# Gathered expert blocks of 64 tokens with two slots each, summed on TensorE as two 64-column tiles

## What is computed

```python
eidx = jnp.take_along_axis(cidx, fi, axis=-1)              # (token, head, 16): rows in u and v
g = jax.nn.softmax(fv, axis=-1)
act = jax.nn.gelu(jnp.einsum('thkd,td->thk', u[eidx], xb).astype(jnp.float32), approximate=False)
return jnp.einsum('thk,thkd->td', (g * act).astype(xb.dtype), v[eidx])
```

## Time and profile before

| | us |
|---|---|
| median of 3 runs | 5584.86 (5583.2 to 5591.33) |
| span of the profiled execution | 5599.6 |
| TensorE, VectorE, GpSimd, ScalarE busy | 4306.3, 3537.3, 2480.1, 1216.0 |
| last stage | 4931 to 5593 |

### The profile page before, as it was taken

One profiled execution on the slowest core, in us unless ns is written; L12 is line 12 of the kernel. 1 busy time (PEld: TensorE's weight loads), 2 busy tenths in 40 slices (PEclk: granted clock), 3 DMA queues, 4 the chain that ended last, 5 costly groups with the idle time before them and its releaser, 6 DMA issues. The chain is left out here.

```text
span 5599.6 us, 50197 instructions
## 1 busy us (share of the span) xinstructions
PE 4306.3 (77%) x15868; PEld 2641.6 (47%) x15868; DVE 3537.3 (63%) x7830; ACT 1216.0 (22%) x3039; POOL 2480.1 (44%) x2215
## 2 busy tenths in 40 slices
PE   7956886578577988689677676968678798767777
PEld 6334775543333765263334565554344476223333
DVE  4055638866677546686666848966667754854544
ACT  2042311121332112120422311121242211111111
POOL 0000010166555544546565332456555554477776
PEclk9975997689789999799898888988889899888888
DMA  4311631389787987889889966688888798799999
GB/s 141 118 60 41 229 124 61 118 294 349 269 272 267 334 284 272 278 308 371 290 292 323 339 203 199 203 286 323 306 274 274 264 359 281 249 361 409 409 409 361
DMA packets 579390, 1484.67 MB, mean 265 GB/s; under 512 B 60104, under 2 KB 251176, under 8 KB 572616
## 3 DMA queue, kind: packets, MB, share of 16 engines
q0 software_dynamic: 307200, 1115.82, 55.2%
q1 hardware_dynamic: 258968, 331.39, 17.8%
q10 hardware_dynamic: 12960, 34.26, 1.6%
HBM read 1435.37 MB, written 45.93 MB: 265 GB/s over the span
## 5 line engine op out<-in xcount | busy, mean ns | idle before, releaser
L2721 PE MATMUL duo<-vring,diag 128*128 128x512 f32 (+1 forms) x2976 | 1509.2, 657 | 401.1 <-DMA vring<-in_peer_v,eidx 173.2
L2593 POOL DMA_INDIRECT uring<-in_peer_u,eidx x981 | 1140.5, 1163 | 1112.3 <-DVE uring L2629 658.0
L2674 POOL DMA_INDIRECT vring<-in_peer_v,eidx x1024 | 1134.0, 1107 | 1067.0 <-PE duo L2721 472.7
L2721 PEld LDWEIGHTS duo<-vring,diag 128*128 128x128 f32 (+1 forms) x2976 | 589.6, 208 | 1197.3 <-issue 944.6
L2629 DVE SCALAR_TENSOR_TENSOR uring<-uring,xr 128x1024 f32<-128x1024 f32 x795 | 958.9, 1221 | 204.6 <-DMA uring<-in_peer_u,eidx 178.8
L689 PE MATMUL duo<-wx,xT 128*128 128x512 f32 (+3 forms) x1440 | 605.1, 578 | 32.9 <-PEq L133 32.1
L2754 DVE SCALAR_TENSOR_TENSOR x_tok<-vring,wt,x_tok 128x1024 f32<-128x1024 f32 x296 | 385.0, 1301 | 97.0 <-DMA vring<-in_peer_v,eidx 70.4
L2702 ACT ACTIVATE diag<-ident,wt 128x128 f32<-128x128 f32 x728 | 269.8, 395 | 748.4 <-PE duo L2721 678.8
L689 PEld LDWEIGHTS duo<-wx,xT 128*128 128x128 f32 (+1 forms) x1440 | 238.9, 176 | 385.8 <-issue 383.1
L2629 DVE SCALAR_TENSOR_TENSOR uring<-uring,duo 128x1024 f32<-128x1024 f32 x201 | 245.4, 1221 | 264.4 <-DMA uring<-in_peer_u,eidx 263.9
L533 PE MATMUL duo<-xT,wx 128*128 128x264 f32 (+1 forms) x1536 | 357.6, 397 | 36.5 <-ACT newcols L556 30.6
(11 more groups left out here) (472 smaller groups left out, 5283.8 us busy)
## 6 DMA issues: line engine op xcount, KB each, us to landing
wx<-in_w_in SPq DMA_DIRECT2D x32, 2048.0 KB
wx<-in_w_in SPq DMA_DIRECT2D x48, 1024.0 KB, 8.3
wm<-in_w_in SPq DMA_DIRECT2D x32, 1024.0 KB, 10.4
wm<-in_w_branch_a SPq DMA_DIRECT2D x32, 1024.0 KB, 11.6
wq<-in_peer_wq SPq DMA_DIRECT2D x32, 1024.0 KB, 8.7
tokm<-tout ACTq DMA_DIRECT2D x64, 256.0 KB
eb<-decays SPq DMA_DIRECT2D x32, 512.0 KB, 4.5
s_h<-in_state_ssm SPq DMA_DIRECT2D x16, 1024.0 KB, 8.3
```

The costliest lines, as they stand in the source:

```text
L2593: pool.indirect_dma_start(out=E.rings.urows[K % E.ur], out_offset=None, in_=table, in_offset=bass.IndirectOffsetOnAxis(ap=E.tiles[q][3][:, ...
L2674: pool.indirect_dma_start(out=E.rings.vrows[K % E.vr], out_offset=None, in_=table, in_offset=bass.IndirectOffsetOnAxis(ap=E.tiles[q][3][:, ...
L2721: mm = pe.matmul(G.bank[6 + c][0:m, :], G.diag[:, R % DR, 0:m], E.rings.vrows[K % E.vr][:, c * BANK:(c + 1) * BANK], start=first, stop=las ...
```

## The change

A gathered block now holds 64 tokens and two of their slots: partition 64k + t has token t of the half tile and its slot number k of the pair. The two blocks that follow each other serve tokens 0 to 63 and 64 to 127 of the tile, so there are as many gathers of the same size as before. The matrix that TensorE multiplies with has 64 columns (`subsel`, two identities one above the other, scaled by the weights), which adds the two slots; the first block of a pair writes PSUM partitions 0 to 63, the second 64 to 127. A pair is issued at once, waits for both of its blocks, and frees them together. All sums are made so; `SHARES`, L2754 and the copies of the token rows into PSUM are gone. The indices and gates are dealt to this layout by four DMAs per tile behind each route (`routed`), and the token rows are loaded as two buffers of 64 tokens each held twice, both used by every tile. The samples' 8 slots keep their layout.

```diff
-UR, VR, DR = 5, 4, 4
+UR, VR = 5, 4
+PACK = 2
+SUB = P // PACK
+DEAL = SLOTS // PACK
+DR = 2 * PACK
...
+        @block.sync
+        def _(sp):
+            go = G.beside.by(sp, "SP")
+            G.ahead.fetch(sp, 0, *vectors)
+            for i, (t, n, heads, sc) in enumerate(units):
+                go(ends[i])
+                sp.wait_ge(sem("routed"), i + 1)
+                if t < NT:
+                    for j in range(PACK):
+                        for k in range(PACK):
+                            sp.dma_start(G.routed[k * SUB:(k + 1) * SUB, t, :, j * DEAL:(j + 1) * DEAL],
+                                         B.dealing[j * SUB:(j + 1) * SUB, :, k * DEAL:(k + 1) * DEAL]).then_inc(sem("dealt"), 16)
+                else:
+                    for a in range(PK // deals):
+                        sp.dma_start(G.eidx_s[a:P:PK // deals, :], S.es[:, 0, a * deals:(a + 1) * deals]).then_inc(sem("dealt"), 16)
+                        sp.dma_start(G.gate_s[a:P:PK // deals, :], S.gs[:, 0, a * deals:(a + 1) * deals]).then_inc(sem("dealt"), 16)
+            sp.wait_ge(sem("dealt"), dealt[-1])
...
+    def column(self, j):
+        return j % PACK * DEAL + j // PACK if self.dealt else j
+
+    def out(self, j):
+        return slice(j % PACK * SUB, (j % PACK + 1) * SUB) if self.dealt else slice(0, self.n)
...
@@ -2603,11 +2641,13 @@
 
     G = E.G
     for q, tile in enumerate(E.tiles):
-        if q >= 2:
-            yield E.first[q - 1] + 0.5
-        if E.k0 or q >= 2:
-            sp.wait_ge(G.dotted, E.k0 + (E.first[q - 1] if q >= 2 else 0))
-        sp.dma_start(G.xr[:, q % 2, :], tile[6]).then_inc(G.xrow[q % 2], 16)
+        for b, rows in zip(tile.buffers, tile.subs):
+            at = E.before(q, b)
+            if at is not None:
+                yield at + 1.5
+            if E.k0 or at is not None:
+                sp.wait_ge(G.dotted, E.k0 + (0 if at is None else at + 1))
+            sp.dma_start(G.xr[:, b, :], rows).then_inc(G.xrow[b], 16)
 
 
...
-            K = E.r0 + i
-            if j == 0:
-                dve.wait_ge(G.xrow[q % 2], 16 * (E.xr0[q % 2] + q // 2 + 1))
-            xr = G.xr[:, q % 2, :]
-            if q in E.copies and i >= E.copied:
-                xr = G.duo[q % 2][:].rearrange("p c n -> p (c n)")
-                dve.wait_ge(E.row_copied, E.copies.index(q) + 1)
+            tile = E.tiles[q]
+            K, b = E.r0 + i, tile.buffer(j)
+            if j < len(tile.buffers):
+                dve.wait_ge(G.xrow[b], 16 * E.loads(q, b))
             dve.wait_ge(E.rings.usems[K % E.ur], 16 * (K // E.ur + 1))
             row = E.rings.urows[K % E.ur]
-            dve.scalar_tensor_tensor(row, row, 1.0, xr, ALU.mult, ALU.mult,
+            dve.scalar_tensor_tensor(row, row, 1.0, G.xr[:, b, :], ALU.mult, ALU.mult,
                                      accum_out=G.pre[:, q % 2, j:j + 1]).then_inc(G.dotted, 1)
         if i - WEIGH_AFTER in E.ends:
             q, lo, hi = E.ends[i - WEIGH_AFTER]
+            tile = E.tiles[q]
             g = E.g0 + E.rank[(q, lo, hi)]
             dve.wait_ge(G.gelu, g + 1)
-            dve.tensor_tensor(G.wt[:, q % 2, lo:hi], G.pre[:, q % 2, lo:hi], E.tiles[q][4][:, lo:hi], ALU.mult).then_inc(G.weighed, 1)
+            dve.tensor_tensor(tile.slots_of(G.wt[:, q % 2], lo, hi), tile.slots_of(G.pre[:, q % 2], lo, hi), tile.gates_of(lo, hi),
+                              ALU.mult).then_inc(G.weighed, 1)
 
 
...
 
     G = E.G
-    copies = {max(E.first[q] - 3.7, E.copied + 0.3): q for q in E.copies}
-    for at in sorted([i + 1.0 for i in E.ends] + list(copies)):
-        yield at
-        if at in copies:
-            q = copies[at]
-            act.wait_ge(G.xrow[q % 2], 16 * (E.xr0[q % 2] + q // 2 + 1))
-            if q >= 2:
-                act.wait_ge(G.dotted, E.k0 + E.first[q - 1])
-            act.activation(G.duo[q % 2][:, 0, :], G.xr[:, q % 2, 0:BANK], ACT.Copy)
-            act.activation(G.duo[q % 2][:, 1, :], G.xr[:, q % 2, BANK:], ACT.Copy).then_inc(E.row_copied, 1)
-            continue
-        i = int(at) - 1
+    for i in sorted(E.ends):
+        yield i + 1.0
         q, lo, hi = E.ends[i]
         act.wait_ge(G.dotted, E.k0 + i)
         act.activation(G.pre[:, q % 2, lo:hi], G.pre[:, q % 2, lo:hi], ACT.Gelu).then_inc(G.gelu, 1)
...
 def sums_scalar(act, E):
 
     G = E.G
-    for v in range(E.n):
-        if not E.on_pe[v]:
-            continue
-        yield max(v + 1.0 - LEAD, E.ready(v))
-        q, j = E.slots[v]
-        K = E.p0 + E.rank_pe[v]
-        act.wait_ge(G.weighed, E.g0 + E.group(q, j) + 1)
-        if K >= DR:
-            act.wait_ge(G.summed, K - DR + 1)
-        sel = E.tiles[q][5]
-        m = sel.shape[1]
-        act.activation(G.diag[:, K % DR, 0:m], sel, ACT.Copy, scale=G.wt[:, q % 2, j:j + 1]).then_inc(G.diagged, 1)
+    for v in range(0, E.n, PACK):
+        yield max(v + PACK - LEAD, E.ready(v))
+        for i in range(v, v + PACK):
+            q, j = E.slots[i]
+            K = E.k0 + i
+            act.wait_ge(G.weighed, E.g0 + E.group(q, j) + 1)
+            if K >= DR:
+                act.wait_ge(G.summed, (K - DR) // PACK + 1)
+            sel = E.tiles[q].sel
+            act.activation(G.diag[:, K % DR, 0:sel.shape[1]], sel, ACT.Copy, scale=G.wt[:, q % 2, j:j + 1]).then_inc(G.diagged, 1)
 
 
 def sums_tensor(pe, E):
 
     G = E.G
-    for v in range(E.n):
-        if not E.on_pe[v]:
-            continue
-        yield v + 1.0
-        q, j = E.slots[v]
-        m = E.tiles[q][5].shape[1]
-        R, K = E.p0 + E.rank_pe[v], E.r0 + v
-        first, last = v == E.pe_first[q], v == E.pe_last[q]
-        if first and E.q0 + E.pe_tiles.index(q) > 0:
-            pe.wait_ge(G.xadd, E.q0 + E.pe_tiles.index(q))
-        pe.wait_ge(G.diagged, R + 1)
-        pe.wait_ge(E.rings.vsems[K % E.vr], 16 * (K // E.vr + 1))
+    for v in range(0, E.n, PACK):
+        yield float(v + PACK)
+        q, j0 = E.slots[v]
+        tile = E.tiles[q]
+        m = tile.sel.shape[1]
+        if j0 == 0 and E.q0 + q > 0:
+            pe.wait_ge(G.xadd, E.q0 + q)
+        pe.wait_ge(G.diagged, E.k0 + v + PACK)
+        for i in range(v, v + PACK):
+            K = E.r0 + i
+            pe.wait_ge(E.rings.vsems[K % E.vr], 16 * (K // E.vr + 1))
         for c in range(2):
-            mm = pe.matmul(G.bank[6 + c][0:m, :], G.diag[:, R % DR, 0:m], E.rings.vrows[K % E.vr][:, c * BANK:(c + 1) * BANK],
-                           start=first, stop=last, skip_group_check=True)
+            for i in range(v, v + PACK):
+                j = E.slots[i][1]
+                mm = pe.matmul(G.bank[6 + c][tile.out(j), :], G.diag[:, (E.k0 + i) % DR, 0:m],
+                               E.rings.vrows[(E.r0 + i) % E.vr][:, c * BANK:(c + 1) * BANK],
+                               start=j < (PACK if tile.dealt else 1), stop=j >= tile.slots - (PACK if tile.dealt else 1), skip_group_check=True)
         mm.then_inc(G.summed, 1)
 
 
 def sums_vector(dve, E):
 
     G = E.G
-    for v in range(E.n):
-        q, j = E.slots[v]
-        t, n = E.tiles[q][0:2]
-        K = E.r0 + v
-        last = v == E.pe_last.get(q)
-        if E.on_pe[v] and not last:
-            continue
-        yield v + 1.0
-        done = E.d0 + E.rank_dve[v]
-        if done:
-            dve.wait_ge(G.folded, done)
-        if last:
-            dve.wait_ge(G.summed, E.p0 + E.rank_pe[v] + 1)
-            if E.q0 + E.pe_tiles.index(q):
-                dve.wait_ge(G.xadd, E.q0 + E.pe_tiles.index(q))
-            for c in range(2):
-                xs = G.x[0:n, t, c * BANK:(c + 1) * BANK]
-                add = dve.tensor_tensor(xs, xs, G.bank[6 + c][0:n, :], ALU.add)
-            add.then_inc(G.xadd, 1)
-        else:
-            added = E.q0 + sum(E.pe_last[p] < v for p in E.pe_tiles)
-            if added and E.pe_last.get(q, v) < v:
-                dve.wait_ge(G.xadd, added)
-            dve.wait_ge(E.rings.vsems[K % E.vr], 16 * (K // E.vr + 1))
-            x = G.x[0:n, t, :]
-            dve.scalar_tensor_tensor(x, E.rings.vrows[K % E.vr], G.wt[:, q % 2, j:j + 1], x, ALU.mult, ALU.add).then_inc(G.folded, 1)
+    for q, tile in enumerate(E.tiles):
+        v = E.first[q] + tile.slots
+        yield float(v)
+        dve.wait_ge(G.summed, E.p0 + v // PACK)
+        if E.q0 + q:
+            dve.wait_ge(G.xadd, E.q0 + q)
+        for c in range(2):
+            xs = G.x[0:tile.n, tile.t, c * BANK:(c + 1) * BANK]
+            add = dve.tensor_tensor(xs, xs, G.bank[6 + c][0:tile.n, :], ALU.add)
+        add.then_inc(G.xadd, 1)
 
 
 DOTS = {"POOL": dots_pool, "SP": dots_sync, "DVE": dots_vector, "ACT": dots_scalar}
```

More of the change, by code:

```diff
@@ L2565, in later, with before, loads @@
     def later(self):
-        n = sum(self.on_pe)
-        return (self.k0 + self.n, self.g0 + len(self.ends), self.q0 + len(self.pe_tiles), self.p0 + n, self.d0 + self.n - n)
+        return self.k0 + self.n, self.g0 + len(self.ends), self.q0 + len(self.tiles), self.p0 + self.n // PACK
+    def before(self, q, b):
```

(19 more changed lines are left out.)

128 lines of the change are left out of this document (58 added, 70 removed).

## The result

The changed kernel takes 5920.16 us (5903.87 to 5930.16) against 5588.09 us of the kernel before on the same chip: ratio 1.0588, 95% interval 1.0565 to 1.0610, slower by 332 us. The forecast was 128 us and its range ended at 5810. The sign held; the size and the range didn't.

What follows compares the result with a forecast made beforehand. The prediction took no one engine as the bound throughout: TensorE, VectorE, alternating engines or DMA, by stage. Terms 99 - 72 + 16 + 18 + 72 - 5 = +128 us on 5585 gave 5713 us, range 5610 to 5810.

Steps and rivals of the forecast that it cites:

- What bounds each kind of stage: TensorE bounds late scores and mix; SSD and attention alternate engines on one tile; DMA bounds the last stage.
- the pair at 1.91 us: On TensorE, two 64-column tiles run side by side, so the sums of two slots take 1.91 us.
- TensorE stages, +99: Late scores, layer 2's early scores and late mix: all sums on TensorE cost +50, +5 and +44 us.
- Alternating stages, -72: SSD, attention and early mix: less sum work gives -20, -39 and -13, together -72 us, between -45 and -110.
- The sentence on the ring: SSD and attention: a block of four frees only with its pair, so the second gather has one slot less lead.
- Dealing, +16: After routes, SyncE's four small index DMAs hold up the end of four stages by about 4 us each, +16 us.
- Token rows, +18 (0 to 36): Six places where the second token-row load waits for the tile before, 3 us each, +18 us (0 to 36).
- Last stage, +72 for the port: Last stage: dots with both operands in SBUF lengthen GpSimd's gathers, a slot 2.88 us for 2.56, +72 us.
- Rival 1: Last stage: the shared read port costs nothing, as gathers waiting in the DMA engines absorb it; 5641 us, chance 0.12.
- rival 2: Last stage: dots lock into a bad phase with gathers, a slot up to 3.57 us; 5868 us, chance 0.12.
- The tail's -5: End of the last stage: 16 pairs take 28 us on TensorE alone, for 35 us side by side, -5 us.
- Rival 4: Sums on TensorE: the two column tiles run one after the other, 3.62 us a pair; 5916 us, chance 0.06.

Runs made afterwards that it cites:

- x1: The changed kernel with each token-row load written as two plain transfers of 64 rows instead of one [2, 64, 1024] transfer; ratio 1.0307 to the kernel before.
- x4: The kernel before without ScalarE's copies of the token rows to PSUM, so last-stage dots read both operands from SBUF; ratio 1.0009 to the kernel before.
- x5: The changed kernel with plain token-row loads and one row buffer moved from the dot products' ring to the sums' ring (4 to 5); ratio 1.0264.
- x3: The kernel before with all sums on TensorE, each a 128-column sum of its own, none on VectorE; ratio 1.0442 to the kernel before.
- the same-columns run: The changed kernel with plain token-row loads, both slots of a pair writing the same 64 output columns; ratio 1.0905 to the kernel before.

## Why the prediction was right or wrong

- **What bounds each kind of stage** and **the pair at 1.91 us**: right. (One reading was off, without effect: a DMA share of 1.03 isn't the most of that trace, weights reach 1.09 from 1086 to 1090.) In the late scores stage TensorE is busy 96.69 of 97.00 us, 25.2 more than in the earlier trace rows, 1.94 us for each of 13 pairs.

```profile
2148.30:2245.30 97.00, 96.69 (x474) 69.25 (x474) 0.00 (x0) 23.41 (x90) 22.96 (x26) 0.98 0.64 205
```

- **TensorE stages, +99**: +94.6 (late scores 48.6, the early one 4.4, late mix 41.6).
- **Alternating stages, -72**: -40.6, outside the bound of -45 (SSD -12.6 for -20, attention -36.7 for -39, early mix +8.7 for -13). For SSD and attention the mechanism was right and partly taken back by the ring: plain loads with four buffers (`x1`) give -49 in these stages against the kernel without PSUM copies (`x4`, same chip), and with five (`x5`, another chip, one buffer fewer for the dots) -86. In the early mix the sum itself has a gap: it takes 18 sums, 23 us, off VectorE and puts nothing on TensorE for the nine pairs that replace them, 17 us at 1.91. With the same sums on TensorE one by one (`x3`) these stages take 385.9 us for the 381.7 of `x4`.
- **Attention inputs and route stages**, whose sums were costed at 0: wrong. First route +31.6, attention inputs +13.0, the early route +6.9. The sentence on the ring ("gathers start two at a time and the second has one slot less of lead") named the cause, and I weighed it only where foreground work could cover it. It costs most in the first route stages, where TensorE has none. Of their +34.6 us with plain loads the fifth buffer takes 31 away; for the attention inputs and the early route no run separates the ring from the rest.
- **Dealing, +16**: the stage with layer 1's early route, whose sums and dots haven't begun, is 4.1 us longer (156.8 for 152.7 us), the 4 us forecast. In layer 2's, SyncE leaves the stage only 1.7 us behind the other engines, and in the other two it can't be told from the reload. The size fits where it can be read.
- **Token rows, +18 (0 to 36)**: the step that failed. "A load takes 4.6 to 9.8, median 7.1 us" was taken from transfers of 128 rows and applied to one of [2, 64, 1024]. It took 17 to 41 us until the dot that needed it, and it also held up the weights issued behind it ("so no weights wait" was wrong in the late halves' first stages, where the loads stand ahead of them). The term of 18 us cost 168 by its shape alone. With loads as I had costed them the waits are 38.8 us, at the upper end of 0 to 36 even so, and in four places and not six.
- **Last stage, +72 for the port**: wrong, zero. "If dots fall at random" failed ("landings jitter"): they lock to the gathers 0.2 us behind a start, a phase that costs 0.07 us a slot, which the 3% that GpSimd had in hand covers. Rival 1 had the right time for it but the wrong reason, and rival 2 (they lock badly) the right mechanism with the wrong phase. The tail's -5 came: from the last dot to the end of the stage are 34.8 us before and 30.4 after.
- **Rival 4** gives 5916, nearly what was measured, by a mechanism that the same-columns run and the records exclude. A total alone would have confirmed it.

Sum of what the runs separate: 168 for the loads' shape; of the 172 left, +95 in TensorE stages, about -31 in SSD, attention and early mix, +35 in first route stages (31 of it the ring), and about 70 in small parts: the tokens stages (23), the sample group's routes (15), the early route (8), attention inputs (7), and others. Reloads behind the last dot and dealing are among them. These are read from the table and not taken apart by a run. Without the loads' shape the time is 1.0307 x 5585 = 5756 us, inside the range, but by luck: two of the terms in it, the port and the paired ring, were then wrong in opposite directions. No variant came below the kernel before: the 95 us in stages that TensorE bounds remain in each of them.
